# Decay rows spread over the partitions by TensorE and ScalarE in place of a store and eight loads through DRAM

## The chip, the cores and the metric

One NeuronCore of a Trainium2 chip runs one program. The metric is the device time of the whole program in microseconds (us), the median of several executions. The core has five engines with in-order queues of their own: PE (TensorE, matmul), ACT (ScalarE), DVE (VectorE), POOL (GpSimd) and SP (SyncE, which here only issues DMAs). They meet through semaphores.

## The reference

The program is two blocks of a network over 512 tokens of width 1024, in float32. What the change touches lies in the first block, in the attention with forgetting (8 heads of 64; 16 meta tokens stand before the 512, so rows have 528 entries):

```python
fox_log_f = log_sigmoid(ff + fox_f_bias)            # (L, 8 heads)
c = cumsum(log_f, axis=1);  cT = c.transpose(0, 2, 1)
s = einsum('bqhd,bkhd->bhqk', q_i, k) * scale
s = s + (c_i[..., :, None] - cT[:, :, None, :])
s = where(key_pos <= q_pos, s, MASK_VALUE)
p = softmax(s);  o = einsum('bhqk,bkhd->bqhd', p, v)
```

The softmax runs over keys, so the term c_i of the query falls out of it. What is needed is, for each head, the row of minus cT over the 528 keys, added to the scores of all 128 queries of a tile. In the kernel's layout queries are partitions, so this row has to stand in every partition. Beside this attention the block has a recurrence over four heads of 128 (HGRN), an output projection and a feed-forward part; then the second block follows (two layers of attention and feed-forward).

## The kernel before

The first 345 us or so are the stage called "mixers". Four stages j = 0..3 each hold two attention heads (index j, h = 0, 1) and one recurrence head (j). The projections for the next stage, the attention of this one and the recurrence of this one are interleaved in one list of steps (`mixers_steps`). Matmuls against weights are done as three matmuls of split operands (L369 to L371); all other matmuls named here are float32.

What sets the order. `mixers_steps` gives the order on PE. `pipelined` and `place` put a list of "fill" steps (each with a cost in us) between the attention's steps in equal shares of the summed cost; so the cost of one fill step shifts where all others fall. ACT, DVE and POOL get their order from `in_time`: it adds the costs (`MIXERS_COST`) up to a time for each step, and each follow-up of a step is due so many us later (the tables `MIXERS_SCALAR`, `MIXERS_VECTOR`, `MIXERS_GPSIMD`); the follow-ups are sorted by due time. SP follows the list itself. `Spare` gives each step one of the PSUM banks 4 to 7 by the same modelled times; banks 0 to 3 belong to the scores. PE waits in `hold` until the last reader of the bank is done.

Names. For head pair j, "scores j x" is the score tile x = 0..3 (L1041, and the causal mask L1045); DVE's "max" (L1386) takes the scores out of PSUM, subtracts them from the decay row in `K.cjb[h]`, writes the result and its row extremum; ACT's "exp" is L1205, DVE's "inv" L1392, ACT's "share" L1211. "turn" is the transposition of the probabilities (L1056), "values" the product with v (L369 to L371 with names FR, Uh). Of the recurrence: "level n" is four matmuls (L1106) that wait for DVE's "scaled n" (L1475, L1476), which needs ACT's exp (L1289) and DVE's "diff n" (L1467, L1468); DVE's "pick n" (L1482) reads the level's bank. "keys" are five transpositions (L1113, L1117), read by ACT's "kdT" (L1299, L1301). "output" is L1136 and L1137 and waits for pick 7; "sums" is L1143. "turn_gv" is L1090 and L1094 and waits for ACT's copy of gv (L1268). "keep" is L1001.

Step "table" j brings the two rows of head pair j to `K.cjb`. PE, ACT and DVE do nothing for it. SP (L1551 to L1560): for j = 0 it waits until DVE has the rows (`x_decay`), stores them from 8 partitions to DRAM (`decay_rows`), waits for the store, and loads each row into all 128 partitions (2 DMAs of 264 KB). For j = 1, 2, 3 it waits for "max j-1, 3", the last reader of the old rows, and then issues 2 such loads. The same queue fetches the weight chunks (`fetch_chunk`, L382), each after the lower half of the chunk two before it has been made (`wlo`, L405 on POOL or DVE).

## Time and profile before

| | |
|---|---|
| median of 3 runs | 2633.69 us (2631.7 to 2635.16) |
| the profiled execution | 2631.7 us, its span 2630.1 us |
| mean granted clock of TensorE over the span | 0.974 of full speed |
| PE busy | 93% of the span, 14115 matmul records |
| DVE, ACT, POOL busy | 60%, 40%, 12% |
| DMA | 28% of 16 engines' time, 84 GB/s |

Each float32 matmul leaves two matmul records, so a timeline's count is twice that of the program's list. Matmuls overlap: in a run of equal ones the spacing of their starts is what one costs, its own duration is longer by the way through the array. "Idle before" in square brackets is the time the engine stood still before that row, and what released it.

### The profile page before, as it was taken

Reading aid. Unit: us, or ns where it says so; the run is one execution under the profiler, and the core shown is the slowest. Engines: PE = TensorE matmul, PEld = TensorE weight load, DVE = VectorE, ACT = ScalarE, POOL = GpSimd, SP = SyncE. Lnnn points to the kernel's source line nnn. Section 1 sums busy time; section 2 is a strip of 40 time slices with the busy share of each in tenths; the row PEclk is TensorE's granted clock in tenths of the full one; section 3 lists DMA queues with packets and bytes.
Section 4 is the critical chain, followed back from the end, with each engine's and each line's share of the span. In section 5 each row is a group of like instructions: output and inputs, shape, how many; then the busy total and the mean of one; then the engine's idle time right before and its main releaser. Section 6 shows DMA issues by size and latency. Waiting matters only on the chain.

```text
span 2630.1 us, 35882 instructions
## 1 busy us (share of the span) xinstructions
PE 2448.7 (93%) x14115; PEld 2104.6 (80%) x14115; DVE 1568.0 (60%) x3016; ACT 1055.3 (40%) x1872; POOL 327.0 (12%) x231
## 2 busy tenths in 40 slices
PE   7999889999998999998799999999889998999998
PEld 6788777788787878776688888889778776788887
DVE  4576647878867677777756544445544456533334
ACT  5555534223254555555521211113555545422223
POOL 2222100000031221221000000002222322000001
PEclk9999999999998999999899999999989999999999
DMA  4222034545521111111234333331212121232331
GB/s 124 65 57 58 17 128 133 183 152 173 179 69 49 41 33 41 41 33 41 73 97 136 94 115 109 120 115 44 55 45 55 46 53 53 77 109 86 100 109 48
DMA packets 237800, 220.73 MB, mean 84 GB/s; under 512 B 26364, under 2 KB 205346, under 8 KB 237634
## 3 DMA queue, kind: packets, MB, share of 16 engines
q1 hardware_dynamic: 237634, 218.45, 27.3%
q8 instruction: 112, 1.84, 0.3%
q14 instruction: 54, 0.44, 0.1%
HBM read 216.17 MB, written 2.24 MB: 83 GB/s over the span
## 4 chain that ended last, share of the span: by engine, by line
PE 72%; DVE 13%; ACT 7%; issue 5%; DMA 1%; POOL 1%; SPq 0%; DVEq 0%; POOLq 0%; ACTq 0%
PE ps L369 22%; PE ps L370 21%; PE ps L371 21%; DVE FR L533 1%; PE ps L2463 1%; ACT whi L394 1%; ACT FA L2556 1%; PE ps L2915 1%; DVE FA L667 1%; DVE hT L2636 1%; DVE wlo L405 1%; ACT FR L528 1%; DVE FA L2676 1%; ACT FA L2984 1%; PE ps L1106 1%
## 5 line engine op out<-in xcount | busy, mean ns | idle before, releaser
L369 PE MATMUL ps<-Uh,whi 128*128 128x512 f32 (+2 forms) x2544 | 898.1, 353 | 16.3 <-ACT FA L2575 5.9
L370 PE MATMUL ps<-Ul,whi 128*128 128x512 f32 (+2 forms) x2544 | 883.4, 347 | 0.0
L371 PE MATMUL ps<-Uh,wlo 128*128 128x512 f32 (+2 forms) x2544 | 882.7, 347 | 0.0
L369 PEld LDWEIGHTS ps<-Uh,whi 128*128 128x128 f32 x2544 | 486.0, 191 | 83.7 <-issue 17.9
L371 PEld LDWEIGHTS ps<-Uh,wlo 128*128 128x128 f32 x2544 | 485.1, 191 | 59.9
L370 PEld LDWEIGHTS ps<-Ul,whi 128*128 128x128 f32 x2544 | 486.0, 191 | 57.4
L394 ACT ACTIVATE whi<-raw 128x1024 fp32r<-128x1024 f32 (+2 forms) x205 | 296.6, 1447 | 533.6 <-PE ps L371 533.4
L405 DVE TENSOR_TENSOR wlo<-raw,whi 128x2048 fp32r<-128x2048 f32 (+2 forms) x121 | 248.4, 2053 | 263.8 <-ACT whi L394 263.4
L369 PE MATMUL ps<-FR,whi 128*128 128x512 f32 (+1 forms) x864 | 301.3, 349 | 14.7 <-DVE wlo L405 4.8
L370 PE MATMUL ps<-FR,whi 128*128 128x512 f32 (+1 forms) x864 | 298.2, 345 | 0.0
L371 PE MATMUL ps<-FR,wlo 128*128 128x512 f32 (+1 forms) x864 | 297.9, 345 | 0.0
L405 POOL TENSOR_TENSOR wlo<-raw,whi 128x1024 fp32r<-128x1024 f32 x84 | 207.8, 2474 | 611.9 <-ACT whi L394 611.3
L533 DVE TENSOR_TENSOR FR<-ps,FR 128x512 fp32r<-128x512 f32 (+7 forms) x284 | 142.3, 533 | 141.8 <-ACT FR L528 140.7
L2156 POOL TENSOR_TENSOR FA<-FA 128x256 f32<-128x256 f32 x63 | 49.9, 807 | 1379.4 <-ACT FA L2036 1378.3
L528 ACT ACTIVATE FR<-FA 128x512 fp32r<-128x512 f32 x100 | 58.4, 584 | 350.1 <-DVE FA L1831 343.5
L667 DVE SCALAR_TENSOR_TENSOR FA<-FA,cond 128x512 f32<-128x512 f32 x280 | 196.9, 744 | 2.3 <-DMA FA<-in_ada_w_dram 1.1
L369 PEld LDWEIGHTS ps<-FR,whi 128*128 128x128 f32 x864 | 164.2, 190 | 37.9 <-ACT whi L394 4.9
L528 ACT ACTIVATE FR<-ps 128x512 fp32r<-128x512 f32 (+7 forms) x304 | 131.0, 467 | 124.0 <-PE ps L371 76.2
L371 PEld LDWEIGHTS ps<-FR,wlo 128*128 128x128 f32 x864 | 164.1, 190 | 19.9
L370 PEld LDWEIGHTS ps<-FR,whi 128*128 128x128 f32 x864 | 164.3, 190 | 19.4
L369 PE MATMUL ps<-whi 128*128 128x512 f32 (+1 forms) x208 | 86.0, 413 | 47.9 <-DVE hT L3068 28.8
L1831 DVE TENSOR_TENSOR FA<-ps,FA 128x512 f32<-128x512 f32 x88 | 54.8, 623 | 115.9 <-PE ps L371 114.4
(346 smaller groups left out, 2992.1 us busy)
## 6 DMA issues: line engine op xcount, KB each, us to landing
FA<-in_ada_w_dram SPq DMA_DIRECT2D x192, 256.0 KB, 2.8
raw<-in_ffn_w_gate_up_dram SPq DMA_DIRECT2D x44, 1024.0 KB, 5.1
raw<-in_ffn_w_down_dram SPq DMA_DIRECT2D x24, 768.0 KB, 4.5
raw<-in_w_in_dram SPq DMA_DIRECT2D x29, 512.0 KB, 3.9
raw<-in_da_wqkv_dram SPq DMA_DIRECT2D x24, 512.0 KB, 3.7
raw<-in_na_wqkv_dram SPq DMA_DIRECT2D x24, 512.0 KB, 3.8
raw<-in_w_ffn_gate_dram SPq DMA_DIRECT2D x11, 1024.0 KB, 5.4
raw<-in_w_ffn_up_dram SPq DMA_DIRECT2D x11, 1024.0 KB, 5.4
```

What stands on the lines that cost most here:

```text
L369: e.matmul(out, ah, bh, start=start, stop=False)
L370: e.matmul(out, ah, bl, start=False, stop=False)
L371: return e.matmul(out, al, bh, start=False, stop=stop)
L394: e.activation(K.view(K.hi[i % 2], i), K.view(K.raw[i % 2], i), ACT.Copy).then_inc(*K.ev("whi", i))
L405: e.tensor_tensor(K.view(K.lo[i % 2], i), K.view(K.raw[i % 2], i), K.view(K.hi[i % 2], i).bitcast(F32), ALU.subtract).then_inc(*K.ev(by, i))
L528: e.activation(hi, src, ACT.Copy, scale=scale).then_inc(*K.ev(*done))
L533: e.tensor_tensor(lo, src, hi.bitcast(F32), ALU.subtract).then_inc(*K.ev(*done))
L667: e.scalar_tensor_tensor(out=o, in0=wv, scalar=K.cond[:, k, c:c + 1], in1=o, op0=ALU.mult, op1=ALU.add).then_inc(*K.ev("ada", i, c))
L1106: t = e.matmul(o[:, c * P:(c + 1) * P], a[:, c * P:(c + 1) * P], b[:, c * P:(c + 1) * P], start=True, stop=True)
L1831: e.tensor_tensor(mt, K.bank(4 + m % 2)[:, 0:t1 - t0], K.sil[:, m % 2, 0:t1 - t0], ALU.mult).then_inc(*K.ev("f_mul", st, m))
L2156: e.tensor_tensor(acc, acc, K.st_sq4[:, k, :], ALU.add).then_inc(*K.ev("pool_sum", f.st, n, i, z))
L2463: t = e.matmul(K.ps[:, 1024 * mp + c0:1024 * mp + c0 + a1 - a0], q[r:r + 64, q0:q0 + P], k[r:r + 64, a0:a1], start=n == 0, stop=n == 2)
```

## The change

The step "table" becomes work of PE and ACT. PE: for each of the two heads a float32 matmul with 8 rows of contraction, whose stationary operand is one column of the identity repeated 128 times, and whose moving operand is the 8 rows of decays (`K.crow`), so that each of the 128 output partitions is a copy of row 2j + h. 528 columns do not fit one bank of 512, so a head takes 396 columns in a bank of its own, and the last 132 of both heads share a third bank. ACT copies the pieces to `K.cjb` (two copies of 396 columns, two of 132), after "max j-1, 3". DVE's "max" waits for these copies instead of for the DMA. The step has a cost of 1.9 in the list and in the model, where it had 0, and SP's step is gone.

```diff
-                     (0, ("table", m, 0)), (0.9, ("level", j, 5)), (0.9, ("states", j, 0)),
+                     (1.9, ("table", m, 0)), (0.9, ("level", j, 5)), (0.9, ("states", j, 0)),
@@ MIXERS_COST
+ "table": 1.9,
@@ mixers_chain
+    if what == "table":
+        return ("forget", 0, 0), 12.0
@@ fox_tensor
+    elif what == "table":
+        w.wait_ge(*K.at("x_decay", 3))
+        banks = K.xbank["table", j] = [spare(1.6) for _ in range(3)]
+        for h in range(2):
+            o = K.hold(w, banks[h], ("x_cjb", j, h))
+            pick = K.ident[0:8, 2 * j + h:2 * j + h + 1].broadcast_to([8, P])
+            e.matmul(o[:, 0:396].rearrange("p (a b) -> p a b", b=66), pick, K.crow[:, 0:6, :], start=True, stop=True)
+        o = K.hold(w, banks[2], ("x_cjb", j, 3))
+        for h in range(2):
+            pick = K.ident[0:8, 2 * j + h:2 * j + h + 1].broadcast_to([8, P])
+            t = e.matmul(o[:, 132 * h:132 * h + 132].rearrange("p (a b) -> p a b", b=66), pick, K.crow[:, 6:8, :], start=True, stop=True)
+        t.then_inc(*K.ev("x_table_rows", j))
@@ MIXERS_SCALAR
+                 "table": (("table", 0.1),),
@@ fox_scalar
+    elif what == "table":
+        banks = K.xbank["table", j]
+        w.wait_ge(*K.at("x_table_rows", j))
+        w.wait_ge(*K.was("x_max", j - 1, 3, 1))
+        for h in range(2):
+            e.activation(K.cjb[h][:, 0:396], K.bank(banks[h])[:, 0:396], ACT.Copy).then_inc(*K.ev("x_cjb", j, h))
+        for h in range(2):
+            e.activation(K.cjb[h][:, 396:528], K.bank(banks[2])[:, 132 * h:132 * h + 132], ACT.Copy).then_inc(*K.ev("x_cjb", j, 2 + h))
@@ fox_vector, "max"
+        w.wait_ge(*K.at("x_cjb", j, 3))
         for h in range(2):
-            w.wait_ge(*K.at(f"table_in{h}", "x", j))
@@ mixers_sync
-        elif what == "table":
-            if j == 0:
-                w.wait_ge(*K.at("x_decay", 3))
-                e.dma_start(K.crowd.ap().rearrange("g (a b) -> g a b", b=66), K.crow).then_inc(*K.dma("rope_in", "rows"))
-                w.wait_ge(*K.at("rope_in", "rows"))
-                w.wait_ge(*K.at("x_turned", KC - 1))
-            w.wait_ge(*K.was("x_max", j - 1, 3, 1))
-            for h in range(2):
-                rows = bass.AP(K.crowd, (2 * j + h) * 528, [[0, P], [1, 528]])
-                e.dma_start(K.cjb[h], rows).then_inc(*K.dma(f"table_in{h}", "x", j))
```

The lines of the new program are some 2 to 23 higher; its names are those of before. PE around table 1, in the middle of stage j = 0, between "keys" and "level 5". Before:

```order
L1106 MATMUL ps<-raw 128x128 x4
L1113 MATMUL ps<-ident,FA 128x128 x4
L1117 MATMUL ps<-ident,FA 16x128
L1106 MATMUL ps<-raw 128x128 x4
L369 MATMUL ps<-whi,Uh 128x256
```

Now (L1121 is "level", L1128 and L1132 "keys", L1037 and L1041 the new matmuls):

```order
L1121 MATMUL ps<-raw 128x128 x4
L1128 MATMUL ps<-ident,FA 128x128 x4
L1132 MATMUL ps<-ident,FA 16x128
L1037 MATMUL ps<-hT,ident 128x396 x2
L1041 MATMUL ps<-hT,ident 128x132 x2
L1121 MATMUL ps<-raw 128x128 x4
L369 MATMUL ps<-whi,Uh 128x256
```

The four new matmuls stand between "keys" and "level 5". Tables 2 and 3 stand at the same place of stages 1 and 2; table 0 stands between the projections fq 0 and fv 0. DVE at the same place, from "rest" to "max 0 3". Before:

```order
L1488 TENSOR_TENSOR FA<-FA 128x16
L1467 TENSOR_TENSOR raw<-FA 128x128x2
L1468 TENSOR_TENSOR raw<-FA 128x128x2
L1475 TENSOR_TENSOR raw<-raw,FA 128x64x4
L1476 TENSOR_TENSOR raw<-raw 128x64x4
L1491 TENSOR_TENSOR FA<-FA 128x528
L1493 COPY small<-hT 128x3
L1495 TENSOR_TENSOR hT<-hT,raw 128x4x128
```

Now (L1490 and L1491 are "diff", L1409 is "max", L535 the lower half of q, which stood there before too):

```order
L1511 TENSOR_TENSOR FA<-FA 128x16
L1498 TENSOR_TENSOR raw<-raw,FA 128x64x4
L1499 TENSOR_TENSOR raw<-raw 128x64x4
L1514 TENSOR_TENSOR FA<-FA 128x528
L1516 COPY small<-hT 128x3
L1518 TENSOR_TENSOR hT<-hT,raw 128x4x128
L535 SCALAR_TENSOR_TENSOR wlo<-ps,wlo 128x512
L1490 TENSOR_TENSOR raw<-FA 128x128x2
L1491 TENSOR_TENSOR raw<-FA 128x128x2
L1409 ISA FA,stat<-ps,FA 128x528
```

"diff 5" (128x128x2) has moved from before "scaled 4" to directly before "max 0 3". On ACT, the four copies follow "kdT" and stand before "share 0 3". PE at the end of stage 0, from "level 7" on. Before:

```order
L1106 MATMUL ps<-raw,FA 128x128 x4
L1136 MATMUL ps<-FA 128x128
L1137 MATMUL ps<-hT 128x128
...
L1137 MATMUL ps<-hT 128x128
L1041 MATMUL ps<-FR,wlo 128x144 x6
L1045 MATMUL ps<-causal_r,identr_r 128x128 x2
```

Now (L1056 and L1060 are the scores, L1151 and L1152 "output"):

```order
L1121 MATMUL ps<-raw,FA 128x128 x4
L1056 MATMUL ps<-FR,wlo 128x144 x6
L1060 MATMUL ps<-causal_r,identr_r 128x128 x2
L1151 MATMUL ps<-FA 128x128
L1152 MATMUL ps<-hT 128x128
```

The scores of the next head pair have moved ahead of "output"; so in stages 1 and 2. The shares of the fill move three more places in stages 0, 1 and 2: "turn j 0" now stands behind the projection "gv 264" instead of ahead of it, directly before "turn_gv"; "turn j 2" stands behind "level 2" instead of ahead of it; and "turn j 7" stands ahead of the projection "gk". On ACT the split of the next chunk (L394) that stood behind the copy of "turn 3" stands ahead of it. Stage 3 keeps its order.

The banks of the tables, as `Spare` gives them: table 0 takes banks 6, 7 and 4, last read long before; tables 1, 2 and 3 take bank 6, free after the lower half of q (L535), bank 7, free after the first "kdT" copy (L1299), and bank 4. "level 5" takes bank 5, and "values 2" takes bank 4, free after the last copy of the table.

## Rows read from the trace of the kernel before

**Rows 1.** Part 1 of the page: busy time, share, records.

```profile
PE 2448.7 (93%) x14115; PEld 2104.6 (80%) x14115; DVE 1568.0 (60%) x3016; ACT 1055.3 (40%) x1872; POOL 327.0 (12%) x231
```

**Rows 2.** Timeline of SP's queue: start us, us, engine, line, operation, names, count.

```profile
61.90 0.82 SPq L1560 DMA_DIRECT2D FA<-decay_rows  x2
62.77 38.87 SPq L382 DMA_DIRECT2D raw<-in_w_in_dram  x5
105.16 0.82 SPq L1560 DMA_DIRECT2D FA<-decay_rows  x2
114.52 60.76 SPq L382 DMA_DIRECT2D raw<-in_w_in_dram  x7
```

**Rows 3.** The loads of the rows by issue (KB, us to landing).

```profile
FA<-decay_rows SPq DMA_DIRECT2D x8, 264.0 KB, 3.7
```

**Rows 4.** Timeline of DVE: the first "max"; in brackets idle before, releaser.

```profile
67.01 0.31 DVE L1386 CUSTOM_DVE_ANT_0 FA<-ps,FA 128x144 f32<-128x144 f32 x1 [5.53 <-PE ps L1045]
```

**Rows 5.** Timeline of PE: prices of float32 matmuls, "sums" and "level 7".

```profile
129.31 1.02 PE L1143 MATMUL ps<-hT,ones 128*128 128x512 f32 x2
118.14 1.06 PE L1106 MATMUL ps<-raw,FA 128*128 128x128 f32 x8
```

**Rows 6.** Durations of "sums": min, median, max ns of one record.

```profile
L1143 PE MATMUL ps<-hT,ones x8: 592/594/697, 129.3 to 335.1; 128*128 128x512 f32 x8
```

**Rows 7.** Timeline of PE where table 1 is put in.

```profile
104.77 0.27 PE L1117 MATMUL ps<-ident,FA 128*16 128x128 f32 x1
105.96 1.13 PE L1106 MATMUL ps<-raw 128*128 128x128 f32 x8 [0.92 <-DVE raw L1476]
106.84 0.37 PE L369 MATMUL ps<-whi,Uh 128*128 128x256 f32 x1
```

**Rows 8.** Timeline of ACT at the same place.

```profile
105.28 0.72 ACT L1205 ACTIVATE FA<-FA,stat 128x528 f32<-128x528 f32 x1
...
106.00 0.57 ACT L1299 ACTIVATE FA<-ps 128x512 f32<-128x512 f32 x1
106.47 0.25 ACT L1301 ACTIVATE FA<-ps 16x128 f32<-16x128 f32 x1
108.30 0.38 ACT L528 ACTIVATE FR<-ps 64x256 fp32r<-64x256 f32 x1 [1.58 <-PE ps L371]
```

**Rows 9.** Timeline of DVE at the same place.

```profile
98.24 0.41 DVE L1467 TENSOR_TENSOR raw<-FA 128x256 f32<-128x256 f32 x1
...
99.54 1.99 DVE L1475 TENSOR_TENSOR raw<-raw,FA 128x256 f32<-128x256 f32 x1 [0.56 <-ACT raw L1289]
...
103.20 0.68 DVE L535 SCALAR_TENSOR_TENSOR wlo<-ps,wlo 128x512 fp32r<-128x512 f32 x1
...
104.43 0.70 DVE L1386 CUSTOM_DVE_ANT_0 FA<-ps,FA 128x528 f32<-128x528 f32 x1
```

**Rows 10.** Timeline of POOL: two lower halves, one beside table 0, one before table 1.

```profile
60.35 2.39 POOL L405 TENSOR_TENSOR wlo<-raw,whi 128x1024 fp32r<-128x1024 f32 x1 [2.42 <-ACT whi L394]
...
96.78 4.46 POOL L405 TENSOR_TENSOR wlo<-raw,whi 128x1024 fp32r<-128x1024 f32 x1 [8.27 <-ACT whi L394]
```

**Rows 11.** Timeline of PE at the end of stage 0.

```profile
120.52 0.46 PE L1136 MATMUL ps<-FA 128*128 128x128 f32 x2 [1.32 <-DVE FA L1482]
...
122.47 0.56 PE L1041 MATMUL ps<-FR,wlo 64*128 64x144 f32 x6
122.96 0.44 PE L1045 MATMUL ps<-causal_r,identr_r 128*128 128x128 f32 x2
```

**Rows 12.** Timeline of PE where "turn" moves: turn 0 0, turn_gv, level 2.

```profile
72.45 0.44 PE L1056 MATMUL ps<-ident,FA 128*128 128x128 f32 x2 [0.78 <-ACT FA L1211]
76.29 0.66 PE L1090 MATMUL ps<-ident,FA 128*128 128x128 f32 x4 [0.48 <-ACT FA L1268]
...
89.34 0.49 PE L1056 MATMUL ps<-ident,FA 128*128 128x128 f32 x3
90.73 1.13 PE L1106 MATMUL ps<-raw 128*128 128x128 f32 x8 [0.90 <-DVE raw L1476]
```

More of the change, by code:

```diff
@@ L937, in mixers_steps @@
             yield "turn_fv", m, 0
-MIXERS_COST = {"forget": 6, "keep": 0.6, "gq": 5.4, "fq": 5.4, "gate": 5.4, "gk": 3, "gv": 3, "fk": 3, "fv": 3, "turn_gv": 0.7,
+MIXERS_COST = {"forget": 6, "keep": 0.6, "gq": 5.4, "fq": 5.4, "gate": 5.4, "table": 1.9, "gk": 3, "gv": 3, "fk": 3, "fv": 3, "turn_gv": 0.7,
                "turn_fv": 0.7, "level": 0.9, "keys": 0.6, "states": 0.9, "output": 1.7, "sums": 0.9}
@@ L1154 @@
                  "fq": (("q_hi", 0.1),), "fk": (("k_hi", 0.1),), "fv": (("v_out", 0.1),), "turn_fv": (("tv_hi", 0.1),),
-                 "scores": (("exp", 1.2), ("share", 3.8)), "turn": (("t_hi", 0.1),),
+                 "table": (("table", 0.1),), "scores": (("exp", 1.2), ("share", 3.8)), "turn": (("t_hi", 0.1),),
                  "values": (("o_hi", 0.1),),
@@ L3264, in build @@
         m["stat"] = sb("stat", [P, 8, 4])
-        m["crowd"] = nc.dram_tensor("decay_rows", (8, 528), F32, kind="Internal")
         m["rpbd"] = nc.dram_tensor("rpb_rows", (240, 128), F32, kind="Internal")
```

## The prediction

> **What bounds the kernel now.** I read the page's busy shares first: PE is busy 93% of the span and no other engine over 60% [rows 1]. So work that is taken off SP is worth something only where PE or an engine that PE waits for has waited for it, and work that is put on PE costs its full length except where PE stood idle at that place. The second view was the timeline of SP's queue, to see when the rows of the table are stored and loaded and what is fetched behind them [rows 2, 3]. The third was the timeline of PE around each step that the change moves, with the waits in brackets [rows 7, 11, 12]; the fourth ACT and DVE at the same times, because the new matmuls need PSUM banks that these two have to empty [rows 8, 9]. The reader should see that PE in the mixers stage has short waits of up to 1.3 us, all of them for DVE or ACT.
>
> **What goes: the DMAs.** For table 0 the loads are issued from 61.90 us, take 0.82 us to issue and 3.7 us to land [rows 2, 3], so they end at about 66.4; the first "max" starts at 67.01 and was released by PE's scores [rows 4]. They were hidden by 0.6 us. For table 1 the loads are issued at 105.16 and land at about 109.7; the first reader is the max of scores 1 0, which PE issues from 122.47 [rows 2, 11], 13 us later. Tables 2 and 3 repeat table 1. Behind the loads in SP's queue stand the weight fetches. The one at 62.77 follows them directly; the lower half on which it waits runs on POOL until 62.74 [rows 10], so it would not go earlier. The one behind table 1 goes at 114.52, long after the loads. I take all nine DMAs as worth 0. Bounds: 0.6 us lost if ACT's copies came later than the DMA did at table 0, and 0.8 us gained (one pair's issue) if a fetch had been held by it.
>
> **What comes on PE: the matmuls.** The trace has no matmul with 8 rows, so I price by columns. "sums" has two records of 512 columns in 1.02 us, one alone lasts 0.594 [rows 5, 6]: the spacing is 0.43 us. "level 7" has 8 records of 128 columns in 1.06 us at 0.275 each, a spacing of 0.112 [rows 5, 7]. Both give 0.84 ns a column and record. A head's 396 columns are two records of 0.33, so 0.66 us; the 132 columns of a head are two of 0.11, so 0.22 us. One table is 2 x 0.66 + 2 x 0.22 = 1.77 us, four tables 7.1 us. Bounds: by the 128-column row alone, taken for each of the four matmuls, 0.9 us a table; by whole 512-column rows for each, 3.4 us. I take 1.77, which both rows support.
>
> **Table 0** stands between two projections without a wait on either side, and its banks have been free for long. It costs its 1.8 us. ACT's copies (about 1.2 us, priced below) lie beside the next projection, 24 matmuls that need another bank.
>
> **Tables 1 to 3.** PE ends "keys" at 105.04 and starts "level 5" at 105.96, after 0.92 us of wait [rows 7]; the same wait stands in each of the three stages. The new matmuls begin in that wait, so 0.92 of the 1.77 us would be free. But the banks come late. The first head's bank is free after the lower half of q, at 103.88 [rows 9]: no wait, 105.04 to 105.7. The second head's bank is free after the first "kdT" copy. That ends at 106.57, because ACT does it behind both exps of tile 3, the second at 105.28 [rows 8], and these wait for DVE's max, the second at 104.43 [rows 9]. Now "diff 5" (two instructions, from 98.24 to 98.98, so 0.7 us) stands directly ahead of the max, where the stretch it has left ends in a wait of 0.56 us for ACT and a 1.99 us "scaled 4" that ran a little past POOL's end at 101.24 [rows 9, 10], so nothing before it gets earlier. Max, exps and kdT come 0.7 later: 107.27. PE then does the second head until 107.95 and the two short pieces until 108.2, and "level 5" starts at 108.2 instead of 105.96: 2.2 us late.
>
> Then "values 2" needs the bank of the short pieces, which ACT frees with its last copy. The copies' price: 0.57 us for 512 columns, 0.25 for 128 [rows 8], with starts 0.47 apart behind the long one; I estimate 0.4 + 0.4 + 0.15 + 0.25 = 1.2 us, bounds 0.6 (four short ones, pipelined) and 2.0 (four long ones). They start when the last matmul is through, about 108.3, and end at 109.5. "level 5" ends its 0.88 us at 109.1, so "values 2" starts at 109.55 instead of 106.84 [rows 7]: 2.7 us late. For three tables 8.1 us. Behind it ACT had 1.58 us of idle time before its next row [rows 8], so share and the copies of "values" are not made late by more than PE is. The bounds for a table: 0.85 (no bank wait at all) and 3.5 (copies at their upper bound).
>
> At this place one rule of the Trainium skill bears on the sum. The row: POOL's 4.46 us at 96.78 is 2.39 long at 60.35, and DVE's "scaled 4" of 0.41 us shape took 1.99, until POOL's end [rows 9, 10]. The Trainium skill, "SBUF — State Buffer", section "SBUF: two separate sides", says that VectorE with two SBUF inputs and GpSimd take one port pair in turn as an exclusive lock for a whole instruction. ACT's split now stands ahead of one copy, so POOL would start about 0.4 us earlier, by the copies' price above. By the rule POOL then takes the pair before DVE's diffs, for 2.4 us, and DVE's chain is not earlier; if the engines did not exclude each other, DVE would be 0.4 us earlier at max, and the sum lower by 3 x 0.4. The trace agrees with the lock, and the sum above, made from the rows without it, stands.
>
> **What the moved steps are worth.** Scores ahead of "output": PE waited 1.32 us there for pick 7, and the scores last 122.47 to 123.35, about 0.9 [rows 11]. They fill the wait: 0.9 gained in each of three stages, 2.7 us (bounds 0 and 1.32 each). "turn 0 0" behind gv 264: its wait of 0.78 for share goes, since a projection now lies before it, and its 0.35 us lie inside turn_gv's wait of 0.48 [rows 12]: 1.1 us. In stages 1 and 2 only the second part, 0.35 each, is there: 0.7. "turn 2" behind "level 2": it lay beside a 0.90 wait of "level 2" for DVE, whose chain begins with the scores and not with PE's turn; "level 2" stays where it is and turn's 0.35 us come on top [rows 12]: 3 x 0.35 = 1.05 lost. "turn 7" ahead of gk takes over gk's wait for the same bank: 0.
>
> **The sum**: 1.8 + 8.1 - 2.7 - 1.1 - 0.7 + 1.05 = 6.4 us. Nothing later in the program absorbs it: the next stages are fed by PE's own results, and their loads follow the same events. The profiled execution took 2631.7 us (span 2630.1 and 1.6 around it), so it would be 2638.1; the median of the runs lies 2.0 above it, so 2640.1 us.
>
> **The rivals.**
> A. The costs come, the gains do not: DVE, pushed back by "diff 5", delivers pick 7 and the scaled operands late, so that PE waits at "output" and the levels as before, behind the scores. Then 1.8 + 8.1 + 1.05 = 11 us: 2644.7. For it: every wait of PE in the stage but two kinds is for DVE. Against: DVE has idle time between each of these, and "output"'s wait is the latency of a level's last pick.
> B. The banks do not bind: exps and kdT come in time, because ACT and DVE settle earlier against a PE that is later. Then the tables are 1.77 + 3 x 0.85 = 4.3, less 3.5 of moves, 0.9 us: 2634.6, no measurable change. Against: kdT's 106.57 stands on the trace, and PE is not later at that point of stage 0 than it was.
> C. The other side: the moves win. If the scores fill all of the 1.32 us in three stages (4.0), "level 2" waits no longer, and the turns give 1.8, against 4.3 of tables, it is 1.5 us less than before: 2632.2. It decides from the point at which a table costs under 1.5 us net. For it: the waits are there. Against: it needs the bank waits gone and the scores longer than they are.
> D. The DMAs did cost something. For a gain the trace would need a wait for them on some engine; DVE's first max was released by PE. At most 0.8 us a table by the queue's issue time; 2637.
>
> **How the numbers follow.** A measurement of this kernel can tell about 0.2%, 5.3 us: above 2639.0 is slower, below 2628.4 faster. Forecast 0.55, own range 2637.5 to 2642.5; A 0.17; B 0.18; C 0.06; D 0.04. Of the forecast's range somewhat over two thirds lie above 2639.0, with the sum just above that line: slower 0.39 + A 0.17 = 0.56. Same: 0.16 of the forecast, B, D and most of C, 0.41. Faster would take three times what C gives: 0.03. The range reaches down into B and up to A's value: 2635 to 2645.
>
> **What would show it.** Right: 32 more matmul records; new records of 396 columns spaced 0.33 us; PE waiting about 1.5 us for ACT's kdT inside tables 1 to 3, and about 0.5 before "values 2" for ACT's last copy; "level 5" without a wait for DVE; "output" with about 0.4 instead of 1.3 us of wait; the first "max" released by PE's scores. Wrong: no waits inside the tables (B), waits for DVE at "output" of over 1 us behind the scores (A), or records of 8 rows that cost other than their columns. A granted clock that falls in the mixers stage where it did not before would break the whole sum.

## The result and the profile after

| | before | after |
|---|---|---|
| median of 4 runs each | 2634.43 us (2631.7 to 2637.01) | 2667.88 us (2665.56 to 2672.69) |
| profiled execution, its span | 2631.7, 2630.1 us | 2657.69, 2655.9 us |
| mean granted clock over the span | 0.974 | 0.965 |

The ratio is 1.0116, 95% interval [1.0098, 1.0135]: slower, as forecast, but by 33 us where the forecast was 6. A trace is of one execution; that of the kernel after took 10 us less than its median, so the traces show 26 of the 33 us. First the page of the kernel after, busy time by engine; it answers to [rows 1].

```profile
PE 2474.9 (93%) x14147; PEld 2127.4 (80%) x14147; DVE 1564.7 (59%) x3016; ACT 1060.6 (40%) x1888; POOL 321.1 (12%) x231
```

There are the 32 new matmul records, but PE is busy for 26 us more, and they should be 7. The work of every matmul is the same, so some of it ran slower. To see where, I cut the mixers stage at "turn_gv" (L1090, now L1105) of each stage j and at its end. Columns: the stretch, its length, busy time and count for PE, PEld, DVE, ACT, POOL, then the granted clock, DMA share, GB/s. Before:

```profile
0.00:76.29 76.29, 58.02 (x386) 53.10 (x387) 30.57 (x77) 41.63 (x82) 17.94 (x12) 0.98 0.43 121
76.29:149.91 73.62, 68.92 (x485) 60.97 (x485) 48.06 (x113) 40.25 (x91) 18.85 (x7) 1.00 0.22 58
149.91:223.33 73.42, 68.98 (x485) 60.98 (x486) 47.89 (x113) 40.24 (x91) 18.84 (x7) 1.00 0.21 59
223.33:297.44 74.11, 70.12 (x496) 61.83 (x496) 47.59 (x113) 40.49 (x92) 18.83 (x7) 1.00 0.17 44
297.44:339.99 42.55, 34.93 (x214) 29.40 (x213) 29.43 (x77) 21.49 (x49) 0.00 (x0) 0.88 0.15 50
```

After, the same five pieces:

```profile
0.00:80.44 80.44, 62.93 (x394) 57.14 (x394) 30.02 (x75) 42.52 (x84) 17.93 (x12) 0.94 0.39 108
80.44:159.43 78.99, 72.78 (x493) 63.44 (x494) 47.27 (x113) 41.41 (x96) 16.78 (x7) 0.98 0.18 47
159.43:242.84 83.41, 77.30 (x493) 67.03 (x494) 46.32 (x113) 41.41 (x95) 16.72 (x7) 0.92 0.18 45
242.84:327.61 84.77, 78.66 (x504) 68.33 (x504) 46.42 (x115) 42.10 (x98) 16.72 (x7) 0.92 0.12 32
327.61:370.37 42.76, 37.32 (x214) 31.59 (x213) 29.41 (x77) 21.62 (x49) 0.00 (x0) 0.80 0.16 50
```

The pieces are 4.2, 5.4, 10.0, 10.7 and 0.2 us longer: 30.4 together; the later stages give 4.6 back, which leaves the span's 25.8. At the lower of TensorE's two levels (granted clock 0.5, 1.2 GHz) the matmuls of a projection start 0.22 us apart where they start 0.12 apart at the upper one (2.4 GHz), nearly twice. So I estimate what the clock costs a piece, where PE is the bound, as the missing share of the clock times the length: 80.44 x 0.06 = 4.8 against 76.29 x 0.02 = 1.5, so 3.3 more in the first, then 1.6, 6.7 and 6.8. That is 18.4 us. (In the last piece, where PE waits a lot, more time at the lower level cost nothing.) What is left is the cost at full clock: 0.9, 3.8, 3.3 and 3.9, so 11.9 us, where the prediction has 6.4.

The result has two parts then: a clock that was forecast not to fall, and 5 us in the sum itself. Four stretches of 6 us in the kernel after show the fall: behind table 0, twice behind table 2, and behind table 3. (Shorter ones lie at 72, 114 and 308 us.)

```profile
60.00:66.00 6.00, 6.00 (x35) 5.58 (x34) 0.59 (x1) 2.17 (x6) 2.38 (x1) 0.72 0.46 123
...
192.00:198.00 6.00, 6.00 (x26) 5.38 (x25) 1.05 (x2) 2.85 (x7) 0.00 (x0) 0.50 0.00 0
198.00:204.00 6.00, 6.00 (x22) 4.78 (x22) 2.18 (x7) 1.96 (x4) 1.55 (x1) 0.50 0.00 0
276.00:282.00 6.00, 5.76 (x27) 5.03 (x26) 1.15 (x2) 2.85 (x7) 0.00 (x0) 0.60 0.00 0
```

At table 0 the fall needs no wait of PE. It comes 1 us behind the matmuls of 8 rows (L1037, L1041), in a projection (L369 to L371), and PE's last wait before them ended at 53.45 us:

```profile
60.53 0.61 PE L1041 MATMUL ps<-hT,ident 8*128 8x132 f32 x4
...
61.91 0.28 PE L369 MATMUL ps<-Uh,whi 128*128 128x264 f32 x1
62.03 0.28 PE L370 MATMUL ps<-Ul,whi 128*128 128x264 f32 x1
...
62.54 0.42 PE L370 MATMUL ps<-Ul,whi 128*128 128x264 f32 x1
62.76 0.42 PE L371 MATMUL ps<-Uh,wlo 128*128 128x264 f32 x1
```

This is PE in the kernel after at table 2, the place of [rows 7] one stage later (start us, us, engine, line, operation, names, tile, count, idle before and its releaser). L1037 and L1041 are the new matmuls, L1121 is "level 5", L369 and L370 are "values 2".

```profile
188.73 0.93 PE L1037 MATMUL ps<-hT,ident 8*128 8x396 f32 x2
191.20 1.04 PE L1037 MATMUL ps<-hT,ident 8*128 8x396 f32 x2 [1.54 <-ACT FA L1322]
192.03 1.08 PE L1041 MATMUL ps<-hT,ident 8*128 8x132 f32 x4
193.05 2.08 PE L1121 MATMUL ps<-raw 128*128 128x128 f32 x8
194.78 0.56 PE L369 MATMUL ps<-whi,Uh 128*128 128x256 f32 x1
```

The wait inside the table is the one that the prediction names, 1.54 us for kdT's copy. Behind it PE is slow: "level 5" takes 2.08 us for what took 1.13 [rows 7].

Now PE's waits from 60 to 340 us, after: who waited, for whom, us in total, times, longest.

```profile
PE ps L1121 <- DVE raw L1499: 5.5, 6, 1.2
PE ps L1037 <- ACT FA L1322: 4.7, 3, 1.6
PE ps L369 <- ACT hT L1332: 3.8, 3, 1.3
PE ps L1071 <- DVE FR L533: 2.3, 3, 0.8
PE ps L1151 <- DVE FA L1505: 1.3, 3, 0.5
PE ps L1105 <- ACT FA L1291: 0.8, 3, 0.3
```

The second, fifth and sixth were forecast. The third was not. It is the projection "gk", which waits for the bank that ACT's ln (L1332) reads. PE around it, in the kernel after (L1158 "sums", L1071 "turn 6", then "turn 7", L369 gk):

```profile
137.62 1.02 PE L1158 MATMUL ps<-hT,ones 128*128 128x512 f32 x2
139.41 0.74 PE L1071 MATMUL ps<-ident,FA 128*128 128x128 f32 x5 [0.77 <-DVE FR L533]
141.43 0.36 PE L369 MATMUL ps<-Uh,whi 128*128 128x264 f32 x1 [1.28 <-ACT hT L1332]
```

and in the kernel before, where "sums" [rows 5] started at 129.31:

```profile
131.11 0.36 PE L369 MATMUL ps<-Uh,whi 128*128 128x264 f32 x1 [0.77 <-DVE FR L533]
...
134.10 0.71 PE L1056 MATMUL ps<-ident,FA 128*128 128x128 f32 x5
```

Why the wait is new: ACT's ln empties the bank of "sums" 3.7 us after "sums" starts, in both kernels. Before, then after:

```profile
132.32 0.67 ACT L1309 ACTIVATE hT<-ps,eps 128x512 f32<-128x512 f32 x1
```

```profile
140.62 0.67 ACT L1332 ACTIVATE hT<-ps,eps 128x512 f32<-128x512 f32 x1
```

In the kernel before, PE comes to gk at 131.11 in a bank that DVE frees, and turn 7 follows at 134.10, when ln is through. Now turn 7 has the first bank and gk starts right behind ln, 141.29.

ACT's copies of the longer pieces (min, median, max ns of one):

```profile
L1219 ACT ACTIVATE FA<-ps x8: 495/498/501, 61.2 to 276.4; 128x396 f32<-128x396 f32 x8
```

### The profile page after: what moved, and what is told of

It reads as the page before. It is cut to its first block, busy times and chain, and to the rows that moved or that the text cites. A ratio compares the mean times of both kernels' runs of the same rounds, so it can differ in the third digit from the quotient of the medians.

```text
span 2655.9 us, 35953 instructions
## 1 busy us (share of the span) xinstructions
PE 2474.9 (93%) x14147; PEld 2127.4 (80%) x14147; DVE 1564.7 (59%) x3016; ACT 1060.6 (40%) x1888; POOL 321.1 (12%) x231
## 4 chain that ended last, share of the span: by engine, by line
PE 73%; DVE 13%; ACT 8%; issue 5%; POOL 1%; SPq 0%; DMA 0%; DVEq 0%; POOLq 0%; ACTq 0%
PE ps L369 23%; PE ps L370 22%; PE ps L371 22%; ACT whi L394 1%; DVE FR L533 1%; PE ps L2476 1%; PE ps L2928 1%; ACT FA L2569 1%; DVE FA L667 1%; DVE hT L2649 1%; ACT FR L528 1%; DVE wlo L405 1%; DVE FA L2689 1%; ACT FA L2997 1%; PE ps L2941 1%
## 5 line engine op out<-in xcount | busy, mean ns | idle before, releaser
L369 PE MATMUL ps<-Uh,whi 128*128 128x512 f32 (+2 forms) x2544 | 899.6, 354 | 17.9 <-ACT FA L2588 5.9
L370 PE MATMUL ps<-Ul,whi 128*128 128x512 f32 (+2 forms) x2544 | 885.2, 348 | 0.0
L371 PE MATMUL ps<-Uh,wlo 128*128 128x512 f32 (+2 forms) x2544 | 884.9, 348 | 0.0
L369 PEld LDWEIGHTS ps<-Uh,whi 128*128 128x128 f32 x2544 | 488.6, 192 | 83.1 <-issue 13.7
L371 PEld LDWEIGHTS ps<-Uh,wlo 128*128 128x128 f32 x2544 | 487.2, 191 | 59.6
L370 PEld LDWEIGHTS ps<-Ul,whi 128*128 128x128 f32 x2544 | 488.5, 192 | 57.2
L394 ACT ACTIVATE whi<-raw 128x1024 fp32r<-128x1024 f32 (+2 forms) x205 | 296.5, 1447 | 530.2 <-PE ps L371 530.0
L369 PE MATMUL ps<-FR,whi 128*128 128x512 f32 (+1 forms) x864 | 301.1, 349 | 14.4 <-DVE wlo L405 4.8
L370 PE MATMUL ps<-FR,whi 128*128 128x512 f32 (+1 forms) x864 | 298.3, 345 | 0.0
L371 PE MATMUL ps<-FR,wlo 128*128 128x512 f32 (+1 forms) x864 | 297.9, 345 | 0.0
L405 POOL TENSOR_TENSOR wlo<-raw,whi 128x1024 fp32r<-128x1024 f32 x84 | 201.5, 2399 | 646.2 <-ACT whi L394 645.5
L369 PEld LDWEIGHTS ps<-FR,whi 128*128 128x128 f32 x864 | 164.2, 190 | 37.1 <-ACT whi L394 4.9
L371 PEld LDWEIGHTS ps<-FR,wlo 128*128 128x128 f32 x864 | 164.2, 190 | 19.8
L370 PEld LDWEIGHTS ps<-FR,whi 128*128 128x128 f32 x864 | 164.3, 190 | 19.3
L369 PE MATMUL ps<-whi 128*128 128x512 f32 (+1 forms) x208 | 86.8, 417 | 48.5 <-DVE hT L3081 28.6
```

The lines of the kernel that those rows point to most:

```text
L369: e.matmul(out, ah, bh, start=start, stop=False)
L370: e.matmul(out, ah, bl, start=False, stop=False)
L371: return e.matmul(out, al, bh, start=False, stop=stop)
L394: e.activation(K.view(K.hi[i % 2], i), K.view(K.raw[i % 2], i), ACT.Copy).then_inc(*K.ev("whi", i))
L405: e.tensor_tensor(K.view(K.lo[i % 2], i), K.view(K.raw[i % 2], i), K.view(K.hi[i % 2], i).bitcast(F32), ALU.subtract).then_inc(*K.ev(by, i))
```

## The experiments

The change has three parts that can be had apart: the matmuls and copies, the order that the cost of 1.9 brings, and within it the place of "diff 5". Two theories of the fall of the clock stood at the start. R: the matmuls that use 8 of the 128 rows make the clock fall. W: the waits do it, whatever the matmuls are. Each run's expectation calls them by its own words. Every ratio is against the kernel before, run beside it on the same chip.

**Full rows.** The new matmuls contract all 128 rows (the other 120 hold zeros), with the same columns, banks and order. The edit also adds one memset on DVE, early in the stage, for the zeros, and the last step of the decay rows waits for it. The lines are shortened; the second pair of matmuls changes alike.

```diff
-            pick = K.ident[0:8, 2 * j + h:2 * j + h + 1].broadcast_to([8, P])
+            pick = K.ident[:, 2 * j + h:2 * j + h + 1].broadcast_to([P, P])
-            e.matmul(..., pick, K.crow[:, 0:6, :], start=True, stop=True)
+            e.matmul(..., pick, K.crow_all[:, 0:6, :], start=True, stop=True)
```

> The changed kernel, but the four matmuls of each table contract over all 128 rows (rows 8 to 127 of the decay rows are set to zero by one memset on DVE early on) instead of 8. Same columns, same order, same banks, same waits. Theory R (rows): matmuls with 8 of 128 rows are what pulled the granted clock down in the mixers stage. It expects the stretches at 0.5 of the clock in the first 340 us, 44 us more than before the change, to fall back to the 17 us of before, and the time to come out near the 2640 us of my own sum, at most 2647. Rival W (waits): the waits inside the tables for kdT (1.6 us, three times) and behind them pulled it down. It expects no change against the changed kernel: 2660 to 2668 us with the low stretches where they were. Rival O (order) expects the same as W.

Measured: 2646.09 us, 1.0048 [1.0032, 1.0064]; the kernel after has 1.0116. Table 2 with full rows (L1038 and L1042 the table, L1122 "level 5"):

```profile
189.80 0.93 PE L1038 MATMUL ps<-hT,ident 128*128 128x396 f32 x2 [1.75 <-ACT FA L1323]
190.57 0.61 PE L1042 MATMUL ps<-hT,ident 128*128 128x132 f32 x4
191.02 1.05 PE L1122 MATMUL ps<-raw 128*128 128x128 f32 x8
```

The wait is even a little longer, 1.75 us, and here the clock stays (1.00 from 192 to 198 us, where it was 0.50). So 18 us (by the ratios) to 22 us (by the medians) of the loss go with the number of rows, and W alone falls. But the clock is not back everywhere:

```profile
138.00:144.00 6.00, 5.49 (x33) 5.53 (x34) 2.92 (x5) 2.65 (x6) 2.31 (x1) 0.72 0.34 89
...
276.00:282.00 6.00, 6.00 (x23) 5.00 (x23) 4.34 (x10) 1.53 (x2) 2.38 (x1) 0.72 0.24 52
```

The first of these falls, and others at 217 and 299 us, come about a microsecond behind PE's wait of 1.28 us for ln before gk (PE goes on at 138.51, 217.85 and 298.85 us); two more lie at 115 and 275 us, some 6 us behind tables 1 and 3. This trace is of the slowest of the four executions, 2653.76 us.

**The order alone.** The kernel before, rows still by DMA, with only the cost and the chain of the step.

```diff
-                     (0, ("table", m, 0)), (0.9, ("level", j, 5)),
+                     (1.9, ("table", m, 0)), (0.9, ("level", j, 5)),
+ "table": 1.9,
+    if what == "table":
+        return ("forget", 0, 0), 12.0
```

> The kernel before with the changed order alone: the table step has its cost of 1.9 in the list and in the model, so all other steps stand where the change puts them, but the rows still come by DMA, PE and ACT do nothing for them, and no PSUM bank is taken. Theory R expects no low clock beyond that of before and my gains of the moved steps, minus 0.7 from 'diff 5' ahead of the max: -2 to -4 us, 2630 to 2633. Rival W expects the same. Rival O expects low stretches in the mixers stage as in the changed kernel and 2645 to 2660 us.

Measured: 2654.52 us, 1.0078 [1.0063, 1.0093]. No matmul of 8 rows is in it, and it loses 20 us, in all four of its runs (2653 to 2660): R alone falls too. PE at "level 5" (L1108) of stages 0 and 1, and the clock behind both:

```profile
109.08 1.61 PE L1108 MATMUL ps<-raw 128*128 128x128 f32 x8 [2.37 <-DVE raw L1478]
...
191.15 1.74 PE L1108 MATMUL ps<-raw 128*128 128x128 f32 x8 [2.36 <-DVE raw L1478]
```

```profile
110.00:116.00 6.00, 6.00 (x26) 5.07 (x24) 1.50 (x3) 1.25 (x3) 0.00 (x0) 0.50 0.14 51
...
192.00:198.00 6.00, 6.00 (x26) 5.27 (x25) 1.29 (x3) 1.31 (x3) 0.00 (x0) 0.50 0.14 52
```

PE waits 1.45 us longer for "scaled 5" than the 0.92 of before, where I had priced the move of "diff 5" at 0.7.

**The matmuls alone.** The kernel after with the order of before: the cost back at 0, the chain out.

```diff
-                     (1.9, ("table", m, 0)), (0.9, ("level", j, 5)),
+                     (0, ("table", m, 0)), (0.9, ("level", j, 5)),
- "table": 1.9,
-    if what == "table":
-        return ("forget", 0, 0), 12.0
```

> The changed kernel with the old order: the table step costs 0 in the list and in the model, the matmuls and copies are there. Theory R: the tables cost what they cost, without the gains of the moved steps and with the low clock: 2660 to 2672 us, low stretches after each table. Rival W: as R, because the bank waits stay. Rival O: 2640 to 2645, low stretches as before the change.

Measured: 2648.19 us, 1.0050 [1.0035, 1.0065]. So the order alone costs about 20 us, the matmuls alone 13, and the two together 33.

**The same with full rows.** Full rows on top of the edit before.

> All four tables by PE and ACT in the old order, contraction over 128 rows. The same with 8 rows took 2648, with low stretches of 3.4 us at 63 us and 10.2 us at 114 us. At full clock the tables cost 3.4 for the first (1.4 of it PE's wait for ACT's last copy) and 2 us for each other, 9.4 in all: 2644. Theory R (8 rows pull the clock down): no low stretch behind the tables, 2641 to 2645. Rival W: low stretches as with 8 rows, 2647 to 2650.

Measured: 2641.80 us, 1.0026 [1.0014, 1.0037], in ten runs all from 2640.64 to 2643.58. The three stages, from turn_gv to turn_gv:

```profile
80.13:155.54 75.41, 70.71 (x493) 62.09 (x494) 48.06 (x113) 41.47 (x95) 18.84 (x7) 1.00 0.19 50
155.54:230.92 75.38, 70.75 (x494) 62.10 (x494) 48.10 (x113) 41.48 (x95) 18.83 (x7) 1.00 0.19 50
230.92:306.93 76.01, 71.88 (x503) 63.03 (x504) 47.77 (x113) 41.74 (x96) 18.82 (x7) 1.00 0.14 36
```

With the clock at 1.00 throughout, a table in a stage costs 75.41 - 73.62 = 1.8 us, then 2.0 and 1.9. The 8 rows cost another 6 us (2648.2 against 2641.8). In the trace with 8 rows the clock is at 0.53 from 114 to 120 us, behind table 1, where PE's wait inside the table is only 0.73 us; with 128 rows that wait is 0.92 us and the clock stays.

**"diff 5" back, rows by DMA.** The order of after, with DVE's "diff 5" again ahead of "scaled 4"; the lines below come on top of the edit of the order alone.

```diff
-    for what, j, x in in_time(mixers_steps(), mixers_cost, MIXERS_VECTOR, mixers_chain):
+    order = in_time(mixers_steps(), mixers_cost, MIXERS_VECTOR, mixers_chain)
+    for jj in range(3):
+        order.remove(("diff", jj, 5))
+        order.insert(order.index(("scaled", jj, 4)), ("diff", jj, 5))
+    for what, j, x in order:
```

> The run of the order alone (rows by DMA), with one thing put back: on DVE 'diff 5' stands again ahead of 'scaled 4', in stages 0 to 2. In the order-alone run PE waited 2.4 us for 'scaled 5' where it waited 0.9 before, three times, and the clock fell to 0.5 right behind two of these waits. Theory D (diff 5 moved makes a wait of 2.4 us, and behind such a wait the clock falls): the waits are 0.9 us again, no low stretch near them, and with my gains of the other moved steps 2629 to 2634 us. Rival P (the turns, scores and 'output' in their new places make the clock fall): stays 2645 to 2655.

Measured: 2636.12 us, 1.0021 [1.0002, 1.0039], against 2654.52 with "diff 5" late. In this order one step on DVE makes 15 us (by the ratios) to 18 us (by the medians) of the 20. PE's wait for "scaled 5" falls from 2.37 us to 1.69 only, not to the 0.9 that I expected; the rest of the order has its part in it. Of the 22.8 us between the two traces 14.7 lie in the four pieces up to the last turn_gv, and 12.3 of these are clock; the other 8.1 lie behind them, where both programs are the same, and are not explained. Also, its ten runs are of two kinds: six from 2631 to 2637 at a mean clock of 0.972 to 0.975, four from 2642 to 2650 at 0.965 to 0.968. Its stages at full clock are 75.34 and 75.21 us, 1.7 and 1.8 above before: the rest of the order is a loss as well. PE's longest waits:

```profile
PE ps L1108 <- DVE raw L1478: 13.9, 13, 1.7
PE ps L369 <- ACT hT L1311: 4.4, 3, 1.5
```

**"diff 5" back, in the kernel after.** The same edit on the kernel after; the wait inside the tables is then under 1 us.

> The changed kernel with 'diff 5' put back on DVE as in the run beside it. The wait for kdT inside tables 1 to 3 gets 0.7 us shorter (1.55 to about 0.85). Theory D+R: of the 33 us the part that the order alone made (about 20) goes, the 8-row matmuls' own part stays: 2645 to 2655. Rival R alone (8 rows make all the low clock): 2658 to 2664, only 3 x 0.7 us less. Rival W (waits inside tables alone): 2640 to 2645.

Measured: 2655.40 us, 1.0076 [1.0053, 1.0099]: 10 to 12 us less than after, not 15 to 18. The low clock behind table 0 is still there (0.80 from 60 to 66 us).

**Both.** "diff 5" back and full rows.

> The changed kernel with both put right: 'diff 5' back ahead of 'scaled 4' and 128 rows of contraction. At full clock its stages cost +0.7 and 3 x 3.0 us over before. Theory D+R (both made the low clock, each a part): 2642 to 2646, a mean clock of 0.971 or more. Rival P (the new order itself stands at the edge of a low clock, as in 4 of 10 runs of the order with diff 5 back): 2646 to 2655.

Measured: 2645.54 us, 1.0045 [1.0028, 1.0062], the same as full rows alone (1.0048). The two cures do not add: once the rows are full, the place of "diff 5" is not measurable. Full rows are worth 8 to 10 us here (1.0076 and 2655.40 without them).

**Behind "states".** The kernel after with tables 1 to 3 two steps later, 8 rows.

```diff
-                     (1.9, ("table", m, 0)), (0.9, ("level", j, 5)), (0.9, ("states", j, 0)),
+                     (0.9, ("level", j, 5)), (0.9, ("states", j, 0)), (1.9, ("table", m, 0)),
```

> The changed kernel with tables 1 to 3 put one place later, behind 'states' and ahead of the gate projection, where the banks are free and ACT has the long projection for its copies. 8 rows of contraction as in the changed kernel. Theory R: the waits for kdT and for the last copy go (about 3 x 2 us, 2660 or a little under), but the low stretches stay, since the 8-row matmuls stay: 2652 to 2662. Rival W: with the waits the low stretches go too: 2636 to 2642 us. Rival O: no forecast of its own but a low clock as in the changed kernel.

Measured: 2644.71 us, 1.0037 [1.0023, 1.0051]. PE's waits from 60 to 340 us in this kernel begin so:

```profile
PE ps L1121 <- DVE raw L1499: 12.8, 12, 2.3
```

None is inside a table any more: its banks are free there. With 8 rows as they are, it is 21 to 23 us better than after. The clock still falls behind table 0, but only shortly behind later tables. So 8 rows were dearer with a wait inside the table than without one.

**Table 0 alone, 8 rows and 128.** The order of before; only table 0 by matmul, the others by DMA. The line shown is one of several; SP's store, and its loads for tables 1 to 3, are back.

```diff
-    elif what == "table":
+    elif what == "table" and j == 0:
```

> The kernel before in its old order, with table 0 alone made by PE (4 matmuls of 8 rows) and ACT, tables 1 to 3 by DMA as before. Table 0 stands between two projections, without a wait before it. My sum for it is +1.8 us. Theory R (8-row matmuls pull the clock down): a stretch at 0.5 begins at about 62 us, right behind the table, and the time is 3 to 5 us over before. Rival N: no such stretch, +1.8 us.

> As the run beside it (table 0 alone by PE, old order), but the four matmuls contract over all 128 rows. Theory R: no stretch at 0.5 at 62 us, +1.8 us over before. Rival N: the same stretch or none in both runs, and the same time in both.

Measured: 2636.11 us, 1.0010 [0.9998, 1.0021] with 8 rows; 2639.28 us, 1.0022 [1.0010, 1.0033] with 128. The traces show what I looked for. With 8 rows, then with 128:

```profile
62.55 0.56 PE L369 MATMUL ps<-Uh,whi 128*128 128x264 f32 x1 [1.42 <-ACT FA L1219]
62.91 0.42 PE L370 MATMUL ps<-Ul,whi 128*128 128x264 f32 x1
```

```profile
62.52 0.36 PE L370 MATMUL ps<-Uh,whi 128*128 128x264 f32 x1 [1.42 <-ACT FA L1220]
62.71 0.28 PE L371 MATMUL ps<-Ul,whi 128*128 128x264 f32 x1
```

The same wait of 1.42 us, which is the last of ACT's copies, and which I had not priced in this order; with 8 rows the projection behind it runs at the lower clock (0.42 us a record), with 128 at the full one (0.28). But the time is not lower with 128 rows, it is 3 us higher: a miss. The traces show why no gain comes of it: with 128 rows the clock falls a little later, to 0.77 from 72 to 78 us, where it is 1.00 with 8. The first piece is 5.1 us longer than before with 8 rows and 5.2 with 128, at a mean clock of 0.96 in both. Here full rows moved the fall and did not prevent it.

**"diff 5" alone, moved late.** The kernel before, with only "diff 5" directly before "max 3".

> The kernel before with one move: on DVE 'diff 5' of stages 0 to 2 stands directly ahead of 'max 3', as in the changed kernel; rows by DMA, all else in the old order. Without any effect on the clock it costs the longer wait of PE for 'scaled 5', 2.4 in place of 0.9 us three times: +4.4 us, 2638 to 2639. Theory D (behind such a wait the clock falls): 'low' stretches of 3 to 14 us near 110, 185 and 260 us, +8 to +18 us in all. Rival E (the clock falls only when PE's new order is there too): +4.4 us and no low stretch there.

Measured: 2638.09 us, 1.0026 [1.0008, 1.0045]; seven runs from 2634 to 2639, three from 2646 to 2658 at a clock of 0.962 to 0.969. A miss: theory D expected 8 to 18 us in all, and it is 3 us by the medians, 7 by the ratios. The waits for "scaled" grow from 10.4 us to 14.4, as they should, 1.3 us a stage, and by the medians there is nothing beyond this:

```profile
PE ps L1106 <- DVE raw L1476: 14.4, 12, 2.3
```

The trace, one of the seven, has this wait three times, 2.25, 2.26 and 2.28 us. The clock falls behind the first (0.74 from 108 to 114 us) and stays at 1.00 behind the other two. So such a wait does not always bring a fall; in all four runs of the new order the loss was there. What the new order adds to it was not taken apart. It has two waits a stage that the old one has not: 1.24 us before "level 2", where it was 0.90 [rows 12], and the 1.3 to 1.5 us before gk.

**Two moves.** The kernel before, rows by DMA, with the two moves that the prediction counts as gains: scores ahead of "output", "turn j 0" behind gv 264.

```diff
+    for j in range(3):
+        s.remove(("scores", j + 1, 0))
+        s.insert(s.index(("output", j, 0)), ("scores", j + 1, 0))
+        s.remove(("turn", j, 0))
+        s.insert(s.index(("turn_gv", j, 0)), ("turn", j, 0))
```

> The kernel before, rows by DMA, with only those two of the changed kernel's moves that I had priced as gains: the scores of the next head pair ahead of 'output', and 'turn j 0' behind the projection gv 264. The rest of the order as before. My prices: 3 x 0.9 + 1.1 + 0.7 = 4.5 us gained: 2630. Rival G (the wait moves on: to the bank that the projection gk takes over, which ACT empties after 'sums', as seen in the run of the order with diff 5 back, +1.8 us a stage): within 1 us of before. Rival P (low clock): above before.

Measured: 2631.86 us in twelve runs, 0.9991 [0.9981, 1.0000]: about 2 to 3 us less than before, the best kernel of the study, and by my bound of 0.2% no measurable gain. The steps were priced at 4.5.

**All traces by the same working.** The four pieces up to the last turn_gv, in us over the kernel before, and the part of it that the missing share of the clock makes (an estimate, as above). A trace can lie off its kernel's median, so both are given.

| kernel | traced, median | over before | clock | the rest |
|---|---|---|---|---|
| after | 2657.7, 2667.9 | 30 | 18 | 12 |
| full rows | 2653.8, 2646.1 | 22 | 8 | 14 |
| order alone, DMA | 2653.8, 2654.5 | 23 | 16 | 6 |
| matmuls alone | 2648.3, 2648.2 | 17 | 7 | 10 |
| matmuls alone, full rows | 2641.9, 2641.8 | 9 | 0 | 9 |
| "diff 5" back, DMA | 2631.0, 2636.1 | 8 | 4 | 4 |
| "diff 5" back | 2648.9, 2655.4 | 25 | 15 | 11 |
| "diff 5" back, full rows | 2643.3, 2645.5 | 19 | 6 | 13 |
| behind "states" | 2652.7, 2644.7 | 20 | 8 | 12 |
| "diff 5" late alone | 2639.3, 2638.1 | 9 | 5 | 4 |
| two moves | 2629.8, 2631.9 | 0 | 3 | -3 |

At full clock the kernels with all four tables cost 9 to 14 us, whatever their rows. The clock adds 0 to 18, and the two kernels that differ in rows alone differ in it: 18 and 8, 15 and 6, 7 and 0.

## Why the prediction came out as it did

Right in direction, wrong in size: 2667.9 against 2640.1, outside the range.

**What failed first** is a sentence at its end: "A granted clock that falls in the mixers stage where it did not before would break the whole sum." It was named there and had no chance and no price; the sum put the cost of the clock at nothing without a reason. It fell, for 18 of the 30 us of the mixers stage in the trace, and the runs show two things that go with it. Rows: full rows take 18 to 22 us off the kernel after, 8 to 10 off the one with "diff 5" back and 6 off the one in the old order, with the columns, banks and order untouched. Order and waits: the order alone, without any such matmul, loses 20 us, and 15 to 18 of them go with one step of DVE. Neither is a rule by which each fall could be told: behind table 0 the clock falls with 8 rows and no wait near them, and three equal waits of 2.3 us ("diff 5" late alone) have a fall behind the first only. The Trainium skill, "TensorE: Matmul & The Clock Gate", section "A second HAM failure mode: psum-queue depth-cycling", describes a kernel in which PE's short idle times between groups of matmuls make the clock go down and up again. The traces here agree in kind, with falls behind waits of 1.3 to 2.4 us, though not behind all of them; that few rows of contraction add to it is shown by the runs alone.

**What failed in the sum**, 11.9 us at full clock instead of 6.4:

- *The moved steps*, -2.7 - 1.1 - 0.7 + 1.05 = -3.45 us in all. With the rows by DMA and "diff 5" back the three stages are 1.7, 1.8 and 2.0 us longer at full clock and the first piece 1.75 shorter, so +3.8 in all, 7.2 us worse than forecast; the tables came out the difference, about 1.8, cheaper. The step that failed is "turn 7 ahead of gk takes over gk's wait for the same bank: 0". Turn 7 does take over the wait of 0.77 us. But gk then gets the bank of "sums", which ACT's ln empties no earlier than before: 1.28 us more. From "sums" to gk it was 131.11 - 129.31 = 1.80 us, and it is 141.43 - 137.62 = 3.81, with turn 7 inside; turn 7's own slot, about 0.6, is freed further down. So the net is 1.4 a stage, 4.2 of the 7.2 us.
- *The gains of the other moves* are there in the profile: "output" waits 1.3 us in three (0.43 each, forecast 0.4), turn_gv 0.8 in three instead of 1.4. By the last experiment they are worth 2 to 3 us and not 4.5.
- *"diff 5" at 0.7.* With the tables by matmul the wait inside a table is 1.5 us, as forecast, so the size was near enough there. With the rows by DMA and in this order it is 2.37 - 1.69 = 0.7 us of wait, as priced. In the old order the same move costs 1.3.
- *Two slips that change little.* By the prediction's own price the two short pieces take 0.44 us and end at 108.4, not 108.2. And the row of "level 7" gives 0.88 ns a column, not 0.84.

**What held.** Price of a table: forecast 1.8 for table 0, and the first piece is 0.9 us longer at full clock, 0.7 by the sum (1.8 less 1.1 of moved turn). (In the old order table 0 costs 3.8, because PE waits 1.42 us there for ACT's last copy.) In the old order a table in a stage costs 1.8 to 2.0, near the forecast of 2.7 less the 0.7 of "diff 5". ACT's copy was estimated at 0.4 us to the next; it lasts 0.498 for 396 columns, and the next starts 0.39 later. "values 2" was to wait 0.5 us for the last copy; it waited 0.2, once, behind matmuls that ran slow, and 0.44 each time with full rows. The first "max" is still released by PE, in the kernel after:

```profile
70.85 0.31 DVE L1409 CUSTOM_DVE_ANT_0 FA<-ps,FA 128x144 f32<-128x144 f32 x1 [10.26 <-PE ps L1060]
```

So the trace bears out that the DMAs were worth nothing, and the matmul tables had no wait to win back: every one of the nine kernels with them is slower than before or at best the same, from 1.0010 (table 0 alone) to 1.0116.

**The rivals.** A (costs without the gains, 2644.7) is nearest in time, but for the wrong reason: "output" did not wait for DVE, gk waited for ACT. B, C and D fell. None of the rivals had the clock in it, and it was more than all of them. The direction was right for a reason of the sum too, 11.9 us at full clock, but the larger part of the loss came from a term that had been put at nothing.

**Open.** What sets off each single fall. The traces have falls that neither rows nor the waits named here explain: at 68 to 76 us, where PE last waited 0.74 us for "max", in the kernel after and in most of those with the order or "diff 5" changed; and one at 184 us with the two moves, where no wait of PE from 77 to 297 us reaches a microsecond. Why runs of one kernel fall into two groups ("diff 5" back with DMA; "diff 5" late alone), with the same program: there is one trace of each kernel, so the two kinds of run could not be compared. Why the two cures do not add (12 us and 22 us alone, 22 together). The share of each wait within the 18.4 us of clock. And why the three kernels of the new order with "diff 5" back are 8 us shorter than before behind the last turn_gv, where the programs are the same.

## What to carry to other kernels

A transfer that hides is free, and its replacement on the busiest engine costs its length; look first at who waits for the transfer. A step's cost in an order list is an edit of its own: give it a run with the old mechanism before you weigh the new one, since here it was 20 of 33 us, and most of those were one step of DVE behind which PE waited. When PE is the bound and its clock is high, ask what the clock may do behind each new wait of PE and each matmul with few rows, and give the case a price and a chance of its own. When a step takes over another's bank, look at who holds the bank that the other one gets.

## What the runs showed of the hardware

- A float32 matmul with 8 rows of contraction and one with 128 cost the same columns: two records of 396 columns 0.93 us, four of 132 0.61, with either.
- With 8 rows the granted clock fell in places where it stayed at 1.00 with 128: behind table 0 (0.72 against 1.00 from 60 to 66 us; no wait of PE is near it in the kernel after) and behind table 2 (0.50 against 1.00 from 192 to 198 us, with waits of 1.54 and 1.75 us inside the table). Behind tables 1 and 3 it fell with 128 rows too. In time the rows were worth 18 to 22 us (after), 8 to 10 ("diff 5" back), 6 (old order) and nothing (table 0 alone). The kernels of a pair also differ in one memset on DVE.
- A wait of PE of 2.3 us did not always lower the clock: of three equal ones in one trace ("diff 5" late alone) one had a fall behind it.
- At the lower clock a projection's matmuls start 0.22 us apart against 0.12. More time at it cost nothing in the last piece of the mixers stage (0.80 instead of 0.88, length 42.76 against 42.55 us), where PE waits for other engines.
- Executions of one program differ in their mean clock: 0.965 to 0.975 and 2631 to 2650 us in ten runs of one kernel. An average over few runs of such a kernel says little.
